# Second block's attention, two heads at a time: products on halves of the TensorE array, one wide vector operation per pair

## What is computed

```python
# sliding window with a sink: head dim 64, 2 key/value heads for 8 query heads
s = einsum('bnqhgd,bnkhd->bnhgqk', qb, kw) * 64 ** -0.5      # masked to a band of 128
m = maximum(max(s), sink)
p = exp(s - m);  p = p / (sum(p) + exp(sink - m))
o = einsum('bnhgqk,bnkhd->bnqhgd', p, vw)
# latent attention: q and k of 64 + 32 features per head, causal
s = (q_nope @ k_nope + q_rope @ k_rope) * 96 ** -0.5
o = softmax(s) @ v
# then
y = sigmoid(g_a) * (o_a @ w_o_swa) + sigmoid(g_b) * (o_b @ w_o_mla)
x = x + y @ w_out
```

## Time and profile before

| | |
|---|---|
| median of 3 runs | 817.67 us (816.4 to 818.17) |
| the profiled execution | 817.69 us, its span 815.9 us |
| TensorE busy | 801.1 us, 98% |
| VectorE busy | 600.5 us, 74% |
| ScalarE busy | 458.0 us, 56% |
| GpSimd busy | 85.8 us, 11% |
| DMA | 140.97 MB, 173 GB/s in the mean |

### The profile page before, as it was taken

How to read it: one execution, slowest core, us unless ns; L and a number is a source line. 1 busy time by engine, 2 the same in 40 slices (tenths; PEclk the granted TensorE clock), 3 DMA queues, 4 the chain that set the end, 5 groups by cost and what they waited for, 6 DMA issues and landing times.

```text
span 815.9 us, 13489 instructions
## 1 busy us (share of the span) xinstructions
PE 801.1 (98%) x5274; PEld 732.7 (90%) x5274; DVE 600.5 (74%) x777; ACT 458.0 (56%) x615; POOL 85.8 (11%) x94
## 2 busy tenths in 40 slices
PE   8999999999999999999999999999999999999996
PEld 7997888999999899999999899889999888888885
DVE  5994997666567888777787877777787856666663
ACT  6669756555444654444545767677546544444443
POOL 2320231000022100000000450500013000000000
PEclk9999999999999999999999999999999999999999
DMA  8754555434545454555544543333435555555521
GB/s 295 253 186 156 176 204 208 150 112 153 182 180 177 162 212 173 188 198 179 198 161 158 219 177 106 129 130 104 156 132 204 207 176 188 202 184 178 204 103 51
DMA packets 22588, 140.97 MB, mean 173 GB/s; under 512 B 3474, under 2 KB 3730, under 8 KB 6546
## 3 DMA queue, kind: packets, MB, share of 16 engines
q1 hardware_dynamic: 22258, 140.03, 48.3%
q10 hardware_dynamic: 288, 0.36, 0.2%
HBM read 139.33 MB, written 1.05 MB: 172 GB/s over the span
## 4 chain that ended last, share of the span: by engine, by line
PE 79%; DVE 11%; ACT 6%; issue 2%; DMA 1%; SPq 0%; DVEq 0%; ACTq 0%
PE pp L1413 20%; PE pp L1376 14%; PE pp L1378 14%; PE pp L1377 14%; PE pp L1415 10%; DVE wlo L847 4%; ACT whi L466 2%; PE pp L1520 1%; PE pp L1496 1%; DMA raw<-in_slabs 1%; DVE xa L951 1%; PE pp L1483 1%; PE pp L1506 1%; ACT gate L601 1%; PE pp L1495 1%
## 5 line engine op out<-in xcount | busy, mean ns | idle before, releaser
L847 DVE TENSOR_TENSOR wlo<-raw,whi 128x2048 fp32r<-128x2048 f32 x129 | 298.7, 2317 | 118.9 <-ACT whi L466 118.9
L466 ACT ACTIVATE whi<-raw 128x2048 fp32r<-128x2048 f32 x129 | 246.1, 1910 | 87.8 <-PE pp L1378 87.4
L1376 PE MATMUL pp<-ahi,whi 128*128 128x256 f32 x768 | 220.5, 287 | 3.1 <-DVE alo L862 1.8
L1413 PE MATMUL pp<-ahilo,whi 128*128 128x512 f32 x704 | 221.4, 396 | 0.0
L1378 PE MATMUL pp<-ahi,wlo 128*128 128x256 f32 x768 | 217.2, 283 | 0.0
L1377 PE MATMUL pp<-alo,whi 128*128 128x256 f32 x768 | 217.2, 283 | 0.0
L1415 PEld LDWEIGHTS pp<-ahilo,wlo 128*128 128x128 f32 x704 | 132.2, 188 | 31.1
L1376 PEld LDWEIGHTS pp<-ahi,whi 128*128 128x128 f32 x768 | 147.1, 192 | 4.8 <-issue 3.2
L1377 PEld LDWEIGHTS pp<-alo,whi 128*128 128x128 f32 x768 | 147.3, 192 | 0.1
L1378 PEld LDWEIGHTS pp<-ahi,wlo 128*128 128x128 f32 x768 | 147.2, 192 | 0.0
L1415 PE MATMUL pp<-ahilo,wlo 128*128 128x256 f32 x704 | 138.3, 278 | 0.0
(11 more groups left out here) (206 smaller groups left out, 868.1 us busy)
## 6 DMA issues: line engine op xcount, KB each, us to landing
raw<-in_slabs SPq DMA_DIRECT2D x125, 1024.0 KB, 4.8
raw<-in_slabs SPq DMA_DIRECT2D x4, 512.0 KB, 9.3
raw<-in_slabs SPq DMA_DIRECT2D x2, 832.0 KB, 4.9
raw<-in_slabs SPq DMA_DIRECT2D x2, 576.0 KB, 4.7
raw<-in_slabs SPq DMA_DIRECT2D x4, 256.0 KB, 5.8
out<-gg SPq DMA_DIRECT2D x4, 256.0 KB, 2.0
x_res<-in_xT SPq DMA_DIRECT2D x3, 256.0 KB, 6.2
gate<-in_final_norm_g SPq DMA_DIRECT2D x1, 512.0 KB, 5.9
```

The costliest lines, as they stand in the source:

```text
L466: e.activation(whi[slot][:, :], raw[slot][:, :], ACT.Copy).then_inc(hi_ready, 1)
L847: e.tensor_tensor(wlo[slot][:, :], raw[slot][:, :], whi[slot][:, :].bitcast(f32), ALU.subtract).then_inc(lo_ready, 1)
L1376: e.matmul(out, lhs[0], rhs[0], start=first, stop=False, skip_group_check=True)
L1413: e.matmul(out[:, m, :], w[m][0], ACT2[:, k, :], start=k == 0, stop=False, skip_group_check=True)
```

## The change

The SWA and MLA attentions leave `att(step)`, which keeps the first block's heads, and work in pairs: pairs 0 to 3 are SWA, 4 to 7 MLA. Tables say in which slab, counted from the first gate slab, a pair has its scores, the transposes of its probabilities and its values. A pair passes one stage per slab, in most slabs one after the other.

- Scores: for SWA, head 0 of the pair on array rows 0 to 63 and head 1 on rows 64 to 127, product by product in turn, into two banks. MLA keeps its 96 rows.
- Values: each head's 64 value columns go to one half of the array's columns, and the two results to partitions 0 to 63 and 64 to 127.
- VectorE and ScalarE treat both heads in one operation, except for the exponentials, which stay four (two per head).
- The probabilities are scaled by a two-tensor operation with the inverse sums broadcast along the row, in place of an operation with a number per row.
- The buffers: one of transposed q and k for a pair, two of scores and probabilities (written over in place), one of transposed probabilities, one result area.

```diff
-STEPS_AT = [0, 2, 2, 1, 1, 1, 1, 2, 2, 2, 2, 2, 2, 1]
+PAIR_S = {1: 0, 2: 1, 3: 2, 5: 3, 8: 4, 9: 5, 10: 6, 11: 7}
+PAIR_PT = {2: 0, 3: 1, 4: 2, 6: 3, 9: 4, 10: 5, 11: 6, 12: 7}
+PAIR_PV = {3: 0, 4: 1, 5: 2, 7: 3, 10: 4, 11: 5, 12: 6, 13: 7}
...
+        PST2, PSS2 = pp[1], pp[3]
+        PSPT2 = pp[2][:, :, :].rearrange("p b n -> p (b n)")
+        PSPV2 = ps[5][:, SEQ:2 * SEQ]
+        PSCQ = (ps[3], ps[4], ps[3])
+        soft = (sm, pr)
...
             for s in range(S2_GA, FFN2):
-                steps = steps_at(s)
-                for step in steps[:1]:
-                    att(step)
+                scores, probs, values = pairs_at(s)
+                if scores is not None:
+                    pair_turned(scores)
+                if values is not None:
+                    pair_hi(values)
                 if early_att(s) and not late_cut(s):
                     pre(s + 2)
-                for step in steps[1:]:
-                    att(step)
+                if S2_UQ <= s < S2_UKV:
+                    uq_evac(s, 0)
+                if s == S2_UKV:
+                    kv_evac(1)
+                if probs is not None:
+                    pair_probs(probs)
...
+                if late_cut(s):
                     pre(s + 2)
+                if scores is not None:
+                    pair_exp(scores)
...
+            def pair_norm(p):
+
+                e.wait_ge(aE, pair(p))
+                x = soft[p % 2]
+                if p < 4:
+                    link(e.tensor_tensor(sums2[:, :, :], sums2[:, :, :], esink2[:, :, :], ALU.add))
+                link(e.reciprocal(rinv2[:, :, :], sums2[:, :, :]))
+                for h, cols in ((0, slice(0, P)), (1, slice(P, 3 * P))):
+                    r = rinv2[:, :, h:h + 1].to_broadcast([P, 2, P * (h + 1)])
+                    ins = e.tensor_tensor(x[:, 0:2, cols], x[:, 0:2, cols], r, ALU.mult)
+                ins.then_inc(aN, 1)
+
+            def pair_max(p):
+
+                e.wait_ge(aS, pair(p))
+                e.wait_ge(aPT, pair(p) - 2)
+                x = soft[p % 2][:, 0:2, :]
+                mask = masks[:, 1 if p < 4 else 0, :].unsqueeze(1).to_broadcast([P, 2, 3 * P])
+                link(e.tensor_tensor(x, PSS2[:, :, 0:3 * P], mask, ALU.add))
+                e.reduce_max(mx2[:, :, 0], x[:, :, 0:P], AX)
+                link(e.reduce_max(mx2[:, :, 1], x[:, :, P:3 * P], AX))
...
             for s in range(S2_GA, FFN2):
-                steps = steps_at(s)
+                scores, probs, values = pairs_at(s)
                 if s == S2_UKV:
                     kv_evac(0)
-                for step in steps[:1]:
-                    att(step)
+                if values is not None:
+                    pair_lo(values)
+                if probs is not None:
+                    pair_norm(probs)
                 if early_att(s) and not late_cut(s) and s < S2_OUT - 1:
                     pre(s + 2)
-                for step in steps[1:]:
-                    att(step)
...
+                if scores is not None:
+                    pair_max(scores)
...
+            def pair_scores(p):
+
+                e.wait_ge(aTe, pair(p))
+                e.wait_ge(aM, pair(p) - 1)
+                for cols, mine, keys in ((slice(0, P), slice(0, P), slice(0, P)),
+                                         (slice(P, 3 * P), slice(P, SEQ), slice(0, SEQ))):
+                    for i in range(2):
+                        rows, b = (slice(64 * i, 64 * i + 64), 0) if p < 4 else (slice(0, MLA_D), i)
+                        ins = e.matmul(PSS2[:, i, cols], qkT[rows, b, 0, mine], qkT[rows, b, 1, keys], start=True,
+                                       stop=True)
+                ins.then_inc(aS, 1)
+
+            def pair_turn_probs(p):
+
+                e.wait_ge(aN, pair(p))
+                e.wait_ge(aL, pair(p) - 1)
...
+            def pair_values(p):
+
+                e.wait_ge(aPTe, pair(p))
+                for h, mine, keys in ((0, slice(0, SEQ), slice(0, SEQ)), (1, slice(P, SEQ), slice(SEQ, 3 * P))):
+                    for i in range(2):
...
+                        ins = e.matmul(PSPV2[64 * i:64 * i + 64, mine], v, pT[:, i, keys], start=h == 0, stop=h == 1,
+                                       skip_group_check=True)
+                ins.then_inc(aPV, 1)
...
+                        if (i, k) == (0, 0):
+                            for step in steps_at(s):
                                 att(step)
+                            pairs_first(s)
+                        if (i, k) == ((0, 4) if n == 1 else (n // 2, 0)):
+                            pairs_second(s)
```

More of the change, by code:

```diff
@@ L163, in steps_at, with pairs_at @@
 def steps_at(s):
[L165 to L170, removed]
-STEPS_AT = [0, 2, 2, 1, 1, 1, 1, 2, 2, 2, 2, 2, 2, 1]
+    return [s - S_GATE] if S_GATE <= s < S_PR + LAG_PV else []
+PAIR_S = {1: 0, 2: 1, 3: 2, 5: 3, 8: 4, 9: 5, 10: 6, 11: 7}
+PAIR_PT = {2: 0, 3: 1, 4: 2, 6: 3, 9: 4, 10: 5, 11: 6, 12: 7}
+PAIR_PV = {3: 0, 4: 1, 5: 2, 7: 3, 10: 4, 11: 5, 12: 6, 13: 7}
+def pairs_at(s):
+    j = s - S2_GA
+    return PAIR_S.get(j), PAIR_PT.get(j), PAIR_PV.get(j)
 def early_att(s):
@@ L197, in unit_of, with pair @@
 def unit_of(step):
[L199 to L203, removed]
+    return step if 0 <= step < HEADS else None
+def pair(p):
+    return HEADS + p + 1
 def program(nc, t):
@@ L915, in _, with pair_lo @@
+            def pair_lo(p):
+                e.wait_ge(aH, pair(p))
+                e.tensor_tensor(pairs[2][1][:, p, :], PSPV2, pairs[2][0][:, p, :].bitcast(f32),
+                                ALU.subtract).then_inc(aL, 1)
             e.memset(epst[:, :], EPS)
@@ L1496, in att @@
-                    e.matmul(PSS[u % 2][:, P:3 * P], qT[rows, b, P:SEQ], kT[rows, b, :], start=True,
+                    e.matmul(PSS[u % 2][:, 0:P], qT[:, b, 0:P], kT[:, b, 0:P], start=True, stop=True)
+                    e.matmul(PSS[u % 2][:, P:3 * P], qT[:, b, P:SEQ], kT[:, b, :], start=True,
                              stop=True).then_inc(aS, 1)
-                u = unit_of(step - LAG_PT) if step - LAG_PT >= kind_base else None
+                u = unit_of(step - LAG_PT)
                 if u is not None:
@@ L1507, in att @@
                     ins.then_inc(aPT, 1)
-                u = unit_of(step - LAG_PV) if step - LAG_PV >= kind_base else None
+                u = unit_of(step - LAG_PV)
                 if u is not None:
@@ L1525, in merge_ready, with pairs_first, pairs_second @@
+            def pairs_first(s):
+                scores, _, values = pairs_at(s)
+                if scores is not None:
+                    pair_turn(scores)
+                if values is not None:
+                    pair_values(values)
+            def pairs_second(s):
+                scores, probs, _ = pairs_at(s)
+                if scores is not None:
+                    pair_scores(scores)
+                if probs is not None:
+                    pair_turn_probs(probs)
             def merge_ready(block, k):
```

247 lines of the change are left out of this document (119 added, 128 removed).

## The result

| | before | changed | ratio, 95% interval |
|---|---|---|---|
| with the first comparison, 4 runs each | 817.12 us (816.4 to 818.17) | 826.33 us (823.37 to 826.68) | 1.0099 [1.0087, 1.0112] |
| once more (e1_again), 15 and 5 runs | 817.9 us | 825.21 us (824.67 to 826.84) | 1.0100 [1.0085, 1.0114] |

The change makes the kernel 1.0% slower, 7 to 9 us. The direction was forecast; the size was not: the median lies above the range, whose upper end was 824.0. The profiled execution was the shortest of its four, 823.37 us with a span of 821.6.

The account below looks back on a forecast made before the run. TensorE, busy 98% of the span, was taken as the bound. New waits of 10.5 us against about 3, less 4.1 of its own work, gave +3.4; the walk's +3.6 was taken: 821.3 us, range 815.5 to 824.0.

Parts of the forecast that it names:

- The new waits: TensorE waits for paired scores and scaled probabilities from first gates to w_o_mla_2: 10.5 us, against about 3 before.
- The price of the wide operations: VectorE, per pair: two-tensor f32 operations at 1.05 ns an element; mask add 0.95 us, scaling 0.33 + 0.69.
- rival 3: VectorE's maximum and scaling: the second head rides nearly free, later waits vanish; 815.7 us, chance 0.14.
- rival 4: VectorE's wide operations at about half a ns an element, the one-tensor pace; 817.1 us, no change, chance 0.14.
- TensorE's own work: Paired scores and values: -1.2 for fewer row-form visits, +2.3 for column visits, -5.2 for overlap; -4.1 us.
- I take the middle: Overlap of the array halves in 12 tiled blocks: 5.2 us saved, between 0 and 7.9; a block costs 1.17.
- rival 1: Tiled scores and values: the array halves don't overlap, 12 blocks cost 0.44 more each; 823.0 us, chance 0.18.
- The clock: TensorE's clock falls in a wait; four us of work at half pace cost 2; 823.3 us, chance 0.12.
- the walk: One clock followed through the queues from pair 0's scores to the end of w_o_mla_2: 604.5 instead of 600.9, +3.6 us.
- The sum was +3.4: Whole stretch: new waits of 10.5, against about 3 now, less 4.1 of TensorE's own work.

Follow-up runs that it names:

- e1_again: The changed kernel run once more with nothing edited; 825.21 us, 1.0100 of the kernel before.
- all moves: The profile of e7: maxima and casts reordered, plus scaling, pair 3's turn and a ScalarE cast moved, on the changed kernel; 811.33 us.
- e10_fill_sized: The changed kernel with 3, 12, 8 and 16 useless products of ones, sized to fit, in four TensorE stops; 821.47 us, 1.0041 of the kernel before.
- e3: The changed kernel with a pair's mask and maxima ahead of the weight cast in VectorE's queue; 817.32 us, 0.9993 of the kernel before.
- e6: e3 with the weight casts of the two w_uq_2 slabs at the slab's head in both queues; 814.95 us, 0.9961 of the kernel before.
- e7: e6 with scaling ahead of the low part, pair 3's turn one w_ukv_2 group later, ScalarE's cast there between its evacuations; 811.33 us, 0.9919.
- e12_stop_4: e7 with TensorE made to wait for ten small GpSimd operations behind pair 5's transposes, a stop of 4.62 us; 818.52 us.
- e4_later: The changed kernel with pair 3's probabilities turned and its values taken one slab later; 829.5 us, 1.015 of the kernel before.
- e2_fill: The changed kernel with 6, 26, 34 and 17 products of ones ahead of four waits for scaled probabilities, but behind other waits; 835.47 us.
- e5_fill_early: The changed kernel with 7, 25, 32 and 17 products of ones ahead of all waits of the turns, longer than the stops; 832.62 us.

## Why the prediction was right or wrong

The four profiles close into one account. Between the yardstick's ends, in us:

| | before | changed | changed, again | all moves |
|---|---|---|---|---|
| first scores to last values | 97.61 | 103.70 | 105.51 | 90.87 |
| idle by the timeline (stops) | 1.88 (4) | 11.16 (6) | 10.71 (5) | 1.82 (3) |
| 0.16 for each stop | 0.64 | 0.96 | 0.80 | 0.48 |
| the rest | 95.09 | 91.58 | 94.00 | 88.57 |

The last column has no fall, so 88.6 is the work of the new form. It is of another order of the queues, but e10_fill_sized, which keeps the changed kernel's, gives nearly the same: 100.54 less 2.12 of stops, 0.80 and 39 fillers at 0.24 is 88.3. The falls of the two changed profiles are then 3.0 (two) and 5.4 (three). The changed kernel is 95.1 - 88.6 = 6.5 better in its work, 9.6 and 9.0 worse in its stops and 3.0 and 5.4 worse by the clock: +6.1 and +7.9. There are 0.5 more at a merge in `w_out_2` (0.95 from one product's start to the next where there was 0.44).

One more line of the trace of the kernel before, its longest stop, bears on the clock, which stays at 1.00 there:

```profile
131.78 0.63 PE L1483 MATMUL pp<-ident,qk 128*128 128x128 f32 x4 [1.57 <-DVE qk L1030]
```

The forecast's terms, one by one:

- **The new waits**: right. Forecast 0.6, 3.1, 0.3, 3.95, 0.4 and 2.2, 10.5 in all; measured 0.92, 3.20, 0.43, 4.15, 0.29 and 2.17, 11.16 idle by the timeline or 12.1 from start to start. The chain through the casts is the cause, shown by e3, e6 and e7, in which moves in the queues alone shrink the stops step by step, to 0.83 at most. That the wait for pair 3 was two waits, the bank's first, I had not seen.
- **The price of the wide operations**: right. Mask add 0.94, scaling 1.03 in its two parts, both as priced. The free ride (rival 3) and its half (rival 4) are out.
- **TensorE's own work**, "I take the middle, which the two passes suggest": wrong by 2.4 in the kernel's favour. -4.1 forecast, -6.5 measured. The overlap is full: a tiled block takes 0.95 (scores, 0.86 and 0.09 of entry) or 0.89 (values) with its entry, not 1.17. The no-overlap case (rival 1) is out. The sum that followed from the Trainium skill, TensorE: Matmul & The Clock Gate, Part 3, was -6.8, and the trace agrees with it: -6.5.
- **The clock**: here the forecast failed. The sum has no term for it. I held a stop of 0.71 without a fall and a slow start of the kernel against each other and gave the fall 0.12, as a single case of 2 us. In truth each of the three stops over 2 us that the walk itself had found was a candidate: the row of 0.71 said nothing of stops of 2 to 4. The longest stop in the same trace was 1.57, shown above, without a fall either. The rows at the kernel's start did speak of a fall. The 6 in the earlier trace rows counts the products that touch the stretch, not those that start in it; in the timeline eleven start from 1.74 to 4 us, some 0.21 apart, where 0.11 is full pace. That is half pace, as the prediction took it, though by a misreading. Three falls at 1.8 (5.4) are larger than the whole forecast loss of 3.6. The Trainium skill, TensorE: Matmul & The Clock Gate, What's actually happening, says that an idle stretch throttles the array to half; the traces agree on the level, and on the fall in 13 of the 16 stops over 2 us in these profiles.
- The errors work against each other. The sum was +3.4; with -2.4 for the work, +2.1 for the stops (12.1 less 2.5 where 10.5 less 3 stood) and +3.0 for two falls it gives +6.1, the first profile's yardstick. With the second profile's three falls and the merge it is 8.4, and the medians say 7.3 and 9.2. So it was luck that the forecast missed by no more: the work, undervalued by 2.4, hid part of what the stops and the clock added.
- The range ended at 824.0, since it took the clock as one case and the full overlap in none. The direction held because the waits, its largest term, were right.

## What to carry to other kernels

When a change makes steps wider and fewer, read the queues: an operation that is short by itself stands behind a cast of 2.3 us, and two such hops make a stop of TensorE; here one call moved ahead of the cast in one queue was worth 8 us, and with the casts, one scaling and one turn moved too the same change went from 1.0% slower to 0.8% faster. Price a forecast stop of 2 us or more on TensorE at its length plus some 2 us for the slow products behind it: that is what most such stops cost here (1.5 to 2.8 for a fall), though the same stop went without in some executions. To tell the two apart, put useless products of the right length into the stop: the wait stays, the fall goes.

## What the hardware did that was not expected

- Stops and what followed them in the fourteen profiles: there is no fall at stops of 1.5 to 1.6 (at 131 us in each) or shorter, nor at one of 1.74 at 8.4 us (e12_stop_4). A fall came with 2.36, 2.76, 3.35, 4.15, 4.62 and both of 4.13. The others go both ways: 2.17 with a fall twice and without once (e4_later), 2.75 with a fall twice (e2_fill, e4_later) and 2.78 without (e5_fill_early), 3.20 without and 3.21 with one twice. None lies between 1.74 and 2.17. What decides in the mixed cases no run here shows.
- The level is the lower of the two (1.2 of 2.4 GHz), by the granted clock of 0.50 and 0.53 and by the pace: 0.42 for 0.23, 0.32 for 0.18 and 0.21 for 0.12. It lasted some 3 to 7 us. It needn't begin where the stop ends: in e1_again the clock is down (0.62) from 533 to 534, while the stop ends at 534.96, and behind the stop that ends at 590.32 it is down only from 591 on (0.64), behind six turns at full pace.
- The clock's fall is why one kernel with the same stops to 0.02 us took 103.70 and 105.51 between the same two instructions (without the stops 91.6 and 94.0), and so a part of its spread.
- Two heads on the two halves of the array take the time of one for rows (0.86 against 0.85); for columns they take 0.80, where the same products take 1.22 on full columns. It is the same whether their products alternate or come head by head (0.80 and 0.81).
- A product of ones in f32, 128 columns, takes 0.24 us in a row of them: seven show as fourteen records in 1.67 us, each with its own weight load.
